# Mixing a head pair's three units with the values in one go, with a third buffer for turned tiles

## The reference

```
logits = q @ k.T * scale (+ bias), masked beyond the query's chunk of 64
p      = softmax(logits)
out    = p @ v            # for each head; then out @ w_out onto the residual
```

## Time and profile before

| what | us |
|---|---|
| median of 3 runs (1224.37 to 1225.64) | 1225.16 |
| the profiled execution | 1226.64 |
| its span | 1224.8 |
| PE busy over the span | 1205.8 (98%) |
| DVE busy | 764.7 (62%) |
| ACT busy | 545.4 (45%) |
| POOL busy | 170.5 (14%) |
| attention 0 (191.7 to 262.6): PE, DVE, ACT, POOL busy | 69.45, 57.97, 47.36, 45.65 of 70.90 |
| attention 1 (741.8 to 821.1): PE, DVE, ACT, POOL busy | 78.40, 50.75, 48.30, 33.94 of 79.30 |

### The profile page before, as it was taken

The page is one execution under the profiler, slowest core; times in us unless marked ns, Lnnn a source line. Parts: engine busy times, 40 slices in busy tenths (PEclk is TensorE's granted clock), DMA queues, the critical chain, the costliest instruction groups (busy, mean ns, idle before and its releaser), DMA issues.

```text
span 1224.8 us, 17141 instructions
## 1 busy us (share of the span) xinstructions
PE 1205.8 (98%) x6046; PEld 970.9 (79%) x6046; DVE 764.7 (62%) x1344; ACT 545.4 (45%) x896; POOL 170.5 (14%) x239
## 2 busy tenths in 40 slices
PE   9999999999999999999999889999999999999998
PEld 7858886678888888888888876778888888888887
DVE  5588987946766566663336887654766656664334
ACT  5554336745443343432236577643643334333322
POOL 0523436720000000000000524430000000000000
PEclk9999999999999999999999999999999999999999
DMA  7522121212232222213233200004222122212332
GB/s 268 164 88 98 70 96 61 71 52 103 103 121 85 103 103 100 88 52 103 87 101 104 73 19 1 1 35 138 103 104 103 68 103 103 103 51 88 100 101 105
DMA packets 26400, 110.83 MB, mean 90 GB/s; under 512 B 2880, under 2 KB 3264, under 8 KB 19184
## 3 DMA queue, kind: packets, MB, share of 16 engines
q1 hardware_dynamic: 26352, 110.21, 26.2%
HBM read 108.06 MB, written 6.33 MB: 93 GB/s over the span
## 4 chain that ended last, share of the span: by engine, by line
PE 90%; DVE 4%; ACT 2%; issue 1%; POOL 1%; DMA 1%; SPq 0%; DVEq 0%; POOLq 0%; ACTq 0%
PE ps L1911 26%; PE ps L1913 26%; PE ps L1912 26%; PE ps L1683 3%; PE ps L1664 3%; PE ps L1528 3%; PE ps L1520 2%; PE ps L1648 1%; PE ps L1550 1%; DVE hs L1418 1%; POOL probs L553 0%; DVE tok L1441 0%; DMA raw<-in_a_in_wide 0%; ACT h_hi L645 0%; DVE act L1224 0%
## 5 line engine op out<-in xcount | busy, mean ns | idle before, releaser
L1024 DVE TENSOR_TENSOR w_lo<-raw,w_hi 128x1024 fp32r<-128x1024 f32 (+2 forms) x109 | 181.0, 1660 | 255.6 <-ACT w_hi L637 255.6
L1911 PE MATMUL ps<-h_hi,w_hi 128*128 128x512 f32 x704 | 274.2, 390 | 0.0
L1912 PE MATMUL ps<-h_lo,w_hi 128*128 128x512 f32 x704 | 273.9, 389 | 0.0
L1913 PE MATMUL ps<-h_hi,w_lo 128*128 128x512 f32 x704 | 273.9, 389 | 0.0
L637 ACT ACTIVATE w_hi<-raw 128x1024 fp32r<-128x1024 f32 (+2 forms) x120 | 173.0, 1441 | 220.1 <-PE ps L1913 220.1
L1911 PE MATMUL ps<-a_hi,w_hi 128*128 128x512 f32 x480 | 187.7, 391 | 0.6 <-DVE a_lo L1244 0.6
L1912 PE MATMUL ps<-a_lo,w_hi 128*128 128x512 f32 x480 | 186.8, 389 | 0.0
L1913 PE MATMUL ps<-a_hi,w_lo 128*128 128x512 f32 x480 | 186.8, 389 | 0.0
L1912 PEld LDWEIGHTS ps<-h_lo,w_hi 128*128 128x128 f32 x704 | 132.2, 188 | 27.5
L1911 PEld LDWEIGHTS ps<-h_hi,w_hi 128*128 128x128 f32 x704 | 132.1, 188 | 27.4
L1913 PEld LDWEIGHTS ps<-h_hi,w_lo 128*128 128x128 f32 x704 | 132.1, 188 | 27.1
(11 more groups left out here) (199 smaller groups left out, 1478.8 us busy)
## 6 DMA issues: line engine op xcount, KB each, us to landing
raw<-in_f_up SPq DMA_DIRECT2D x44, 1024.0 KB, 4.8
raw<-in_f_w_down SPq DMA_DIRECT2D x44, 512.0 KB, 3.3
raw<-in_a_in_wide SPq DMA_DIRECT2D x12, 1024.0 KB, 4.9
bias_tiles<-bias_rows SPq DMA_DIRECT2D x1, 4096.0 KB, 20.1
raw<-in_a_w_out SPq DMA_DIRECT2D x8, 512.0 KB, 3.3
raw<-in_b_w_out SPq DMA_DIRECT2D x8, 512.0 KB, 3.2
xT<-in_xt SPq DMA_DIRECT2D x8, 256.0 KB, 6.7
raw<-in_a_in_wide SPq DMA_DIRECT2D x8, 256.0 KB, 6.8
```

The costliest lines, as they stand in the source:

```text
L1024: dve.tensor_tensor(w_lo[:, s, 0:n], raw[:, s, 0:n], w_hi[:, s, 0:n].bitcast(F32), ALU.subtract)\
L1911: pe.matmul(dst, s_hi, m_hi, start=start, stop=False)
L1912: pe.matmul(dst, s_hi, m_lo, start=False, stop=False)
L1913: return pe.matmul(dst, s_lo, m_hi, start=False, stop=stop)
```

## The change

PE no longer mixes one unit in each step. It turns the three units of a pair, with the scores between them as before, and then mixes all three. The mix of the last unit of a pair stands directly behind the turn of that unit and the scores of that step. At the end of an attention the first products of the output projection stand ahead of the last three mixes. Since three turned units are then alive at once, there is a third buffer: in attention 0 two free rows of `act`, in attention 1 a tile in space that other tensors (the bias tiles and others) use at other times. The orders of DVE, ACT, POOL and SP are untouched.

```
-        probsT = [sb(f"probsT{j}", [P, 2, S]) for j in range(2)]
+        with ExitStack() as scope:
+            third_b = sb("third_b", [P, 2, S], F32, scope)
         ...
+        turned0, turned1 = sb("probsT0", [P, 2, S]), sb("probsT1", [P, 2, S])
+        probsT = [[turned0, turned1, act[:, 22:24]], [turned0, turned1, third_b]]
...
-                sc.activation(probsT[u % 2][:, e, 0:w], ps[:, turn_bank(u, e), 0:w], ACT.Copy)\
+                sc.activation(probsT[n][u % 3][:, e, 0:w], ps[:, turn_bank(u, e), 0:w], ACT.Copy)\
...
-                dve.tensor_copy(probsT[u % 2][:, e, 0:w], ...)
+                dve.tensor_copy(probsT[n][u % 3][:, e, 0:w], ...)
...
-                                        v[:, kb, h * DH:(h + 1) * DH], probsT[u % 2][:, e, c * P:(c + 1) * P],
+                                        v[:, kb, h * DH:(h + 1) * DH], probsT[n][u % 3][:, e, c * P:(c + 1) * P],
...
                     turn(n, s)
                     if s + 3 < UNITS:
                         scores(n, s + 3)
-                    if s:
-                        mix(n, s - 1)
                     if s == UNITS - 2:
                         early_rows(2 * n, 0)
                     if s == UNITS - 1:
                         early_rows(2 * n, 1)
-                mix(n, UNITS - 1)
+                    if s % 3 == 2:
+                        for u in range(s - 2, s + 1):
+                            mix(n, u)
```

More of the change, by code:

```diff
@@ L1239, in turned_probs @@
                 w = U_COLS[u % 3]
-                dve.tensor_copy(probsT[u % 2][:, e, 0:w], ps[:, turn_bank(u, e), 0:w]).then_inc(pt_dve[n], 1)
+                dve.tensor_copy(probsT[n][u % 3][:, e, 0:w], ps[:, turn_bank(u, e), 0:w]).then_inc(pt_dve[n], 1)
             def act_lo(n, kk, b):
```

## The result

The changed kernel takes 1227.77 us as the median of 12 runs (1226.63 to 1229.45), the kernel before 1225.43 (1224.37 to 1225.68). The ratio is 1.0022 with a 95% interval of 1.0014 to 1.0031: **+2.3 us, slower by a fifth of a per cent**. The forecast was 1228.2 and +3.0.

What follows compares the result with a forecast made beforehand. PE was taken to bound the kernel, holding 90% of the chain. Attention 0's +7.0 - 0.5 and attention 1's -2.5 - 1.0 gave +3.0, so 1228.2 us, range 1224.2 to 1231.2.

Steps and rivals of the forecast that it cites:

- The visits of the mixes: PE, both attentions: a visit costs 0.29 us, visits fall from 24 to 8 each; three mixes together take 2.34.
- The wait in attention 1: PE at the pair's third turn: waits 0.28 us; a pair takes 9.28 instead of 9.59, -2.5 in all.
- the chain from S3 to I2: From a pair's first scores through DVE's logits to its inversion for the third turn: 2.18 us in attention 1.
- The wait in attention 0: PE at the pair's third turn: waits 1.6 us; a pair takes 9.52 instead of 8.35, +7.0 in all.
- B4: DVE's mask_bias ahead of the third turn's inversion, attention 0: 0.74 us as in the first pair, not the steady 0.84.
- Behind the last scores: End of each attention: fewer visits, one mix now standing here, shape switches; -0.5 us in attention 0, -1.0 in attention 1.
- The sum: Whole kernel: 7.0 - 0.5 - 2.5 - 1.0 = +3.0 us, 1228.2 on the median.
- The one that ends faster: Both attentions: the chain hides anyway and PE gains every visit, -8.8 us, 1216.4; chance 0.08.
- The second, that the two cancel: Attention 0's chain is 0.1 to 0.5 us shorter than in the first pair: 1226.3, 1225 to 1227.6; chance 0.22.
- the likeliest case: Whole kernel: attention 0 loses more than attention 1 gains, 1228.2 us, own range 1227.2 to 1229.5; chance 0.60.
- The second wait: The third turn's wait makes something else 0.3 to 0.8 us late a pair, or seams cost 0.15: 1231.5; chance 0.10.
- The signs: Profile after: third-turn waits on POOL about 11 us in attention 0, 2 in attention 1; DVE idle time moves.

Runs made afterwards that it cites:

- the early I2: Changed kernel with DVE's inversion for each pair's third unit issued right behind the copies of the pair's first turn: 1221.63 us against 1225.13 for the kernel before.
- I2 passes B4: Changed kernel with DVE's inversion for the pair's third unit issued ahead of its mask_bias in attention 0: 1225.01 us against 1225.13 for the kernel before.
- POOL's moved bias: Changed kernel with the early I2, plus POOL's bias for third units moved behind its scaling for the third turn: 1218.70 us against 1225.05 for the kernel before.
- three further moves: Each on the early I2 with POOL's moved bias: all DVE mask_bias ahead of logits, 1221.99 us; one behind the second turn's copy, 1220.78; one copy to ACT, 1221.69.

## Why the prediction was right, point by point

- **The visits of the mixes.** Right. Three mixes in one block took 2.33 (2.34 forecast), and no seam between two units costs anything. The third buffer, put at nothing, cost nothing. By the prediction's own sum without waits attention 1 is 9.00 a pair, which the runs with the early I2 show.
- **The wait in attention 1.** Right: 0.26 a pair (0.28), 9.26 (9.28). That the chain from S3 to I2 makes it is shown, as it is gone once I2 leaves that chain.
- **The wait in attention 0.** The mechanism was right and carried the result; its size was 0.2 a pair too large. S3 to S5 took 4.96 (218.86 to 223.82), not 5.16. The term that was mis-sized is B4: I had 0.66 from its start to I2's, from the first pair, and it took 0.47; the pieces ahead of it and behind it came out within 0.01. The prediction said that B4 would run without POOL beside it and took the first pair's 0.74 for that. But there POOL's bias was still at work until 195.60, 0.33 us into B4 (195.27):

```profile
194.69 0.91 POOL L585 TENSOR_TENSOR act<-toep_b,mask 128x384 f32<-128x384 f32 x1 [2.46 <-DMA toep_b<-bias_tiles]
```

In the changed kernel B4 ran with POOL idle and took 0.56. So 0.74 and 0.84 were both lengths with POOL beside it. Over six pairs the 0.2 is 1.2, so attention 0 lost 5.35 and not 6.5. The run in which I2 passes B4 shows that B4 doesn't leave the chain by standing elsewhere: beside N2 it still costs 0.22 of its 0.47.
- **Behind the last scores.** Forecast -0.5 and -1.0; from S23 to the products it was 13.80 instead of 14.24 (-0.4) and 14.84 instead of 15.54 (-0.7). In attention 1 I had taken T22's old wait for POOL of 0.61 as gone. The two turns, now in a row, took 1.81 where their own work is 0.71 + 0.66: about 0.4 of waiting was left.
- **The sum.** -3.36 + 5.35 = +2.0 against +3.0, so the measured +2.3 is nearer to the forecast than the attentions are, and that part is luck. About 0.3 of it comes from the start, where half of the runs of the changed kernel had a lower mean clock (0.998 or 0.999) and only 1 of the 65 comparable runs of the kernel before beside the experiments. With the new order in attention 0 alone it was 2 of 5, in the other variants 1 of 89. Why it differs stays open; the code of that stretch is the same. The 0.36 between the attentions in the profile needs no cause in the change: from the end of attention 0 to the start of attention 1 the thirteen profiled executions took 478.9 to 479.6, and the old and the new order are mixed in that range.
- **The rivals.** The one that ends faster fell by T2's rows. The second, that the two cancel because the chain in attention 0 is 0.1 to 0.5 a pair shorter, was right in its term: it was 0.2 shorter. Its 1225 to 1227.6 and the likeliest case's 1227.2 to 1229.5 both hold the 1227.2 of the runs at full clock, so the result lies at the border of the two. The second wait, of T2 for T1's copy, shows only once the first is gone.
- **The signs.** POOL's waits at the turns were forecast at about 11 us in attention 0 and 2 in attention 1; the view prints 8.7 and 0.9, since the waits of a turn's second head lie within the blocks. DVE's idle time came to T0's copies (0.80) and L3 (0.41) as forecast, but it did not leave L5 (0.74, before 0.66).

## What to carry to other kernels

When work is taken out from between two links of a chain that runs through other engines, count the chain as well as the work: here 1.8 us of mixes (1.03 and 0.81) had covered the way from scores over DVE and POOL to the turn. The repair was not to put them back but to issue one 0.16 us instruction earlier in an in-order queue, since its input had long been there. And where several queues stand within a few tenths of each other, each repair uncovers the next limit: the early I2 and POOL's moved bias helped (5.4 and 2.9 us), and each of three further moves, of which two were expected to give about 2 us and one nothing, cost 2 to 3.

A length taken from a trace holds for what ran beside it there. Before a row is used as the cost of an instruction running alone, look at the other engines in the same stretch.

## What the runs showed of the hardware

- The same DVE tensor_tensor on two SBUF tiles (B4, 128x384) took 0.56 us with POOL idle, 0.74 with POOL's bias work beside it for 0.33 us, 0.84 with 0.42 us, and up to 1.50 where POOL's had begun 0.07 ahead. In other places it kept 0.54 and POOL's work grew: the scaling of 512 columns for both heads took 1.58 when B4 had begun ahead of it, instead of 1.36. The Trainium skill ("SBUF — State Buffer", section Who interferes with whom) says that a DVE instruction with two SBUF inputs contends with a GpSimd instruction that reads SBUF; these rows agree. The prediction had used the rule for a tenth of a microsecond a pair, the difference of two lengths that both held a collision; against the length alone it was 0.18 and 0.28.
- A DVE instruction that reads what the one right ahead of it writes started 0.17 us behind that one's end; others started 0.08 ahead of it.
- Two executions with the same code up to attention 0 differed by 2.36 us there: after 1.86 us of idle PE the products from 8.45 to 11.84 us ran at 1.2 GHz, after 0.27 us of idle they ran at 2.4 GHz. Whether the idle time brought the lower clock was not tried.
